# Key norms and gate sums moved from the chunks of a hybrid recurrent layer into its projection

## What is computed

```
x += 0.5 * post(SwiGLU_1(pre(x)))
h  = pre(x);  z = h @ w_in           # one combined projection
      gated DeltaNet (4 heads of 128), GLA (4 heads), Mamba-2 SSD (8 heads), merge gates
x += post(out(merge of the three branches by sigmoid gates of h))
x += 0.5 * post(SwiGLU_2(pre(x)))
```

```
def _l2norm(x):
    return x * rsqrt(sum(x*x, axis=-1) + 1e-6)
# DeltaNet, per chunk:  G = cumsum(g);  dec = exp(G_i - G_j)
#   A = strict(beta * (k k^T) * dec);  sol = (I + A)^-1 [beta v, beta e^G k]
#   u = sol_v - sol_k S;  o = (q e^G) S + ((q k^T) * dec) u
#   S = e^G_last S + (k e^(G_last - G))^T u
# Mamba-2 SSD: the same running sums, with dt * A as the gate
```

## Time and profile before

| | us |
|---|---|
| median of 3 runs (3424.24 to 3428.06) | 3427.71 |
| the profiled execution | 3428.86 |
| its span, first to last instruction | 3427.1 |
| PE busy | 3229.5 (94%) |
| DVE busy | 1315.3 (38%) |
| ACT busy | 778.4 (23%) |
| POOL busy | 1572.4 (46%) |
| mean granted clock of PE | 0.966 |
| projection of layer 0, its 40 windows and narrow stage | 480 to 711 |
| chunk stage of layer 0 | 711 to 1006 |
| chunk stage of layer 1, its chunks | 2410 to 2706 |

### The profile page before, as it was taken

How to read it: one execution, slowest core, us unless ns; L and a number is a source line. 1 busy time by engine, 2 the same in 40 slices (tenths; PEclk the granted TensorE clock), 3 DMA queues, 4 the chain that set the end, 5 groups by cost and what they waited for, 6 DMA issues and landing times. The chain is left out here.

```text
span 3427.1 us, 67666 instructions
## 1 busy us (share of the span) xinstructions
PE 3229.5 (94%) x26954; PEld 3108.2 (91%) x26954; DVE 1315.3 (38%) x2171; ACT 778.4 (23%) x1447; POOL 1572.4 (46%) x948
## 2 busy tenths in 40 slices
PE   7999989988889999999999999999888899899997
PEld 7999989977669998999999999899676799899997
DVE  3331065558752214331043310753676522233301
ACT  2111032234441112111021111332434311221100
POOL 4665546610016654655545654566000266545553
PEclk9999999998979999999999999999988899999999
DMA  3222222200042222222222222222001322212221
GB/s 124 88 86 85 69 77 86 92 1 1 29 145 87 87 88 68 86 86 85 76 78 88 90 80 69 82 87 73 1 2 70 118 87 90 89 62 86 89 82 65
DMA packets 77997, 259.88 MB, mean 76 GB/s; under 512 B 8576, under 2 KB 10624, under 8 KB 77056
## 3 DMA queue, kind: packets, MB, share of 16 engines
q1 hardware_dynamic: 77536, 256.90, 23.4%
q10 hardware_dynamic: 288, 0.49, 0.1%
HBM read 242.78 MB, written 14.58 MB: 75 GB/s over the span
## 5 line engine op out<-in xcount | busy, mean ns | idle before, releaser
L510 POOL TENSOR_SCALAR wh<-raw 128x1024 fp32r<-128x1024 f32 (+1 forms) x464 | 471.8, 1017 | 1757.3 <-PE ps L551 1161.6
L512 POOL TENSOR_TENSOR wl<-raw,wh 128x1024 fp32r<-128x1024 f32 (+1 forms) x464 | 1066.8, 2299 | 67.8 <-POOL wh L510 0.3
L547 PE MATMUL ps<-hh,wh 128*128 128x272 f32 x4768 | 999.4, 291 | 67.2 <-DVE hl L1767 44.5
L549 PE MATMUL ps<-hl,wh 128*128 128x272 f32 x4768 | 994.0, 289 | 0.0
L551 PE MATMUL ps<-hh,wl 128*128 128x272 f32 x4768 | 989.5, 289 | 0.0
L547 PEld LDWEIGHTS ps<-hh,wh 128*128 128x128 f32 x4768 | 755.9, 190 | 74.9 <-issue 59.3
L549 PEld LDWEIGHTS ps<-hl,wh 128*128 128x128 f32 x4768 | 753.3, 189 | 0.0
L551 PEld LDWEIGHTS ps<-hh,wl 128*128 128x128 f32 x4768 | 752.7, 189 | 0.0
L1776 DVE SCALAR_TENSOR_TENSOR f<-f,prm,rstd_post 128x544 f32<-128x544 f32 x48 | 43.7, 916 | 653.7 <-ACT rstd_post L1276 653.7
L547 PE MATMUL ps<-ah,wh 128*128 128x272 f32 x1408 | 294.5, 291 | 0.0
L549 PE MATMUL ps<-al,wh 128*128 128x272 f32 x1408 | 290.2, 287 | 0.0
(11 more groups left out here) (421 smaller groups left out, 3678.5 us busy)
## 6 DMA issues: line engine op xcount, KB each, us to landing
raw<-in_up SPq DMA_DIRECT2D x176, 512.0 KB, 3.5
raw<-in_win SPq DMA_DIRECT2D x80, 512.0 KB, 3.5
raw<-in_merge SPq DMA_DIRECT2D x96, 384.0 KB, 3.1
raw<-in_down SPq DMA_DIRECT2D x64, 512.0 KB, 3.5
raw<-in_down SPq DMA_DIRECT2D x32, 384.0 KB, 3.2
raw<-in_wout SPq DMA_DIRECT2D x16, 512.0 KB, 3.5
states<-in_in_gdn SPq DMA_DIRECT2D x2, 2048.0 KB, 8.1
proj<-in_in_ssd SPq DMA_DIRECT2D x2, 2048.0 KB, 12.4
```

The costliest lines, as they stand in the source:

```text
L510: pool.tensor_scalar(hi, src, 1.0, 1.0, MULT, MULT).then_inc(hi_done, 1)
L512: pool.tensor_tensor(lo, src, hi.bitcast(F32), SUB).then_inc(lo_done, 1)
L547: pe.matmul(out, high, mh_[:, c], start=a, stop=False)
L549: pe.matmul(out, high, ml_[:, c], start=False, stop=False)
```

## The change

1. `common` is gone from the chunks, with its instructions on PE, ACT and DVE.
2. **Keys and queries** are normalised in the projection, in place. Behind the conv tiles ACT loads its Ln/Exp table and squares the eight tiles (L1713) into rows of `proj` that are still unused; PE adds `key_sums(t)` (L1212) behind window 12 + t, in the PSUM slot that is free then; ACT takes Ln (L1721) and Exp (L1723); DVE multiplies the tiles in place.
3. **Gate sums** of all chunks are made near the projection's end: five transposes behind the first window of group 8 (`token_rows`), the running sums of 512 columns twice behind its third (`running_sums`), the sum rows behind the first of group 9 (`sum_rows`). ACT copies them out.
4. The chunks read `cm`, `tm_all`, `gc` and `rg` by chunk, and the keys and queries from `proj`. DeltaNet's spreads wait for the chunk before (`g_oc`, `g_s`). In the sample step `bx` is made first. The sample norm waits for two more things.
5. The projection's windows are written out from the fourth group on (28 of 40), and the three order strings are new.

The diff, cut to its core:

```diff
@@ PE, chunks
-            def common(step):
-                pe.wait_ge(both["cc"], value(pe, step.once + 1))
-                pe.transpose(ps[0:n, 2, 0:P], cc[:, 0:n], ident).then_inc(both["tmp"], 1)
...
-                for b in range(-(-w // 512)):
-                    c = min(512, w)
-                    last = pe.matmul(ps[:, b, 0:c], ones, sq8[:, b * 512:b * 512 + c], start=True, stop=True)
             def gdn(step):
-                pe.wait_ge(g_["brb"], value(pe, o + 1))
-                pe.wait_ge(both["rg"], further(pe, o + 1))
+                pe.wait_ge(g_["oc"], o + 1)
+                pe.wait_ge(g_["s"], o + 1)
...
@@ PE, projection
+            def key_sums(layer, t):
+                slot = (t + 2) % 4
+                pe.wait_ge(key_["sq"], layer * KEYS + t + 1)
+                pe.wait_ge(evict_done, layer * 40 + 12 + t + 3)
+                for h in range(2):
+                    last = pe.matmul(ps[:, 2 * slot + h, 0:HALF], ones, key_squares(t)[:, h * HALF:(h + 1) * HALF], start=True, stop=True)
+                last.then_inc(key_["ss"], 1)
+            def token_rows(layer):
...
+                for c in range(CHUNKS):
+                    pe.transpose(ps[:, 4, c * P:(c + 1) * P], cm[:, c * P:(c + 1) * P], ident)
+                pe.transpose(ps[0:SAMPLE, 5, 0:P], cm[:, SEQ:T], ident).then_inc(gate_["tr"], 1)
+            def running_sums(layer):
...
+                pe.matmul(ps[:, 0, :], tri, tm_all[:, :], start=True, stop=True)
+                pe.matmul(ps[:, 1, :], rev, tm_all[:, :], start=True, stop=True).then_inc(gate_["cum"], 1)
...
-                with pe.Fori(0, 10) as i:
+                with pe.Fori(0, 3) as i:
                     for j in range(4):
+                        window(i, j)
+                for t in range(KEYS + 2):
+                    if t >= 2:
+                        pe.wait_ge(key_["ln"], layer * KEYS + t - 1)
+                    window(3 + t // 4, t % 4)
+                    if t < KEYS:
+                        key_sums(layer, t)
...
+                window(8, 0)
+                token_rows(layer)
+                window(8, 1)
+                pe.wait_ge(gate_["tm"], layer + 1)
+                window(8, 2)
+                running_sums(layer)
+                window(8, 3)
+                pe.wait_ge(gate_["gc"], layer + 1)
+                window(9, 0)
+                sum_rows(layer)
+                window(9, 1)
+                pe.wait_ge(gate_["br"], layer + 1)
...
@@ ACT, projection
-                with act.Fori(0, 2) as i:
-                    direct_group(i, 3, LQ, ACT.Copy)
+                act.preload_act_table_set(LN_EXP)
+                act.wait_ge(csil_done, layer * CONV_TILES + KEYS + 2)
+                for t in range(2):
+                    square(t)
+                for t in range(KEYS):
+                    block_in(0, 3, t)
+                    act.activation(halves(proj[:, LQ + t, :]), pair(t % 4), ACT.Copy).then_inc(evict_done, 1)
+                    act.wait_ge(key_["ss"], layer * KEYS + t + 1)
+                    act.activation(halves(key_squares(t)), pair((t + 2) % 4), ACT.Ln, bias=epsc).then_inc(key_["ln"], 1)
+                    act.wait_ge(key_["ln"], layer * KEYS + t + 1)
+                    act.activation(key_squares(t), key_squares(t), ACT.Exp, scale=-0.5).then_inc(key_["rs"], 1)
+                    if t + 2 < KEYS:
+                        square(t + 2)
...
@@ DVE, projection
                     conv_group(i, 0, 0)
+                for t in range(KEYS):
+                    dve.wait_ge(key_["rs"], layer * KEYS + t + 1)
+                    dve.scalar_tensor_tensor(out=proj[:, GQ + t, :], in0=proj[:, GQ + t, :], scalar=GDN_SCALE if t < 4 else 1.0,
+                                             in1=key_squares(t), op0=MULT, op1=MULT).then_inc(key_["n"], 1)
                 narrow_columns(layer)
...
@@ DVE, chunks
-                dve.tensor_tensor(view(kn[:, 0:w], 4), proj[:, GK:GK + 4, step.cols], view(rs8[:, w:2 * w], 4), MULT)
-                dve.scalar_tensor_tensor(out=view(qn[:, 0:w], 4), in0=proj[:, GQ:GQ + 4, step.cols], scalar=GDN_SCALE,
-                                         in1=view(rs8[:, 0:w], 4), op0=MULT, op1=MULT).then_inc(g_["qk"], 1)
```

More of the change, by code:

```diff
@@ L679, in spread @@
-            def spread(bank, off, rowi, n):
-                return pe.matmul(ps[:, bank, off:off + n], cst[:, IDENT + rowi:IDENT + rowi + 1].to_broadcast([P, P]),
-                                 br[:, 0:n], start=True, stop=True)
+            def spread(bank, off, rowi, step):
+                return pe.matmul(ps[:, bank, off:off + step.n], cst[:, IDENT + rowi:IDENT + rowi + 1].to_broadcast([P, P]),
+                                 cm[:, step.cols], start=True, stop=True)
             def gdn(step):
@@ L1058, in ssd @@
                 for h in range(SSD_HEADS):
-                    last = spread(6 + h // 4, h % 4 * n, ROW_DT + h, n)
+                    last = spread(6 + h // 4, h % 4 * n, ROW_DT + h, step)
                 last.then_inc(s_["bc"], 1)
@@ L1681, in project @@
                     conv_group(i, 5, SX, 12)
-                for group, tile in ((7, GZ), (8, LG), (9, SZ)):
-                    direct_group(0, group, tile, ACT.Silu)
+                act.wait_ge(key_["n"], layer * KEYS + KEYS)
+                direct_group(0, 7, GZ, ACT.Silu)
+                for t in range(8):
+                    block_in(0, 8, t)
+                    act.activation(halves(proj[:, LG + t, :]), pair(t % 4), ACT.Silu).then_inc(evict_done, 1)
+                    if t == 0:
+                        act.wait_ge(gate_["tr"], layer + 1)
+                        act.activation(tm_all[:, :], ps[:, 4, :], ACT.Copy)
+                        act.activation(tms[0:SAMPLE, :], ps[0:SAMPLE, 5, 0:P], ACT.Copy).then_inc(gate_["tm"], 1)
+                    elif t == 2:
+                        act.wait_ge(gate_["cum"], layer + 1)
+                        for dst, bank in ((gc, 0), (rg, 1)):
+                            for at_, rows in gate_rows:
+                                m = rows.stop - rows.start
+                                last = act.activation(dst[:, 0:CHUNKS, at_:at_ + m],
+                                                      ps[:, bank, :].rearrange("p (c r) -> p c r", r=P)[:, :, rows], ACT.Copy)
+                        last.then_inc(gate_["gc"], 1)
+                    elif t == 4:
+                        act.wait_ge(gate_["row"], layer + 1)
+                        for r in (slice(0, 32), slice(64, P)):
+                            act.activation(cm[r, 0:SEQ], ps[r, 4, :], ACT.Copy)
+                            act.activation(cm[r, SEQ:T], ps[r, 5, P:P + SAMPLE], ACT.Copy)
+                        for at_, rows in gate_rows:
+                            m = rows.stop - rows.start
+                            last = act.activation(gc[0:SAMPLE, CHUNKS, at_:at_ + m], ps[0:SAMPLE, 5, rows], ACT.Copy)
+                        last.then_inc(gate_["br"], 1)
             def narrow_columns(layer):
@@ L1706, in _ @@
                 act.preload_act_table_set(LN_EXP)
+                act.wait_ge(gate_["gc"], layer + 1)
+                act.activation(rg[:, :, :], rg[:, :, :], ACT.Exp).then_inc(gate_["rg"], 1)
                 steps = steps_of(layer)
[L1708 removed]
+                together(SCALAR_ORDER, g=branch_of(gdn, gdn_sample, steps),
                          l=branch_of(gla, gla_sample, steps), s=branch_of(ssd, ssd_sample, steps),
@@ L2341, in sample_norm @@
                 dve.wait_ge(s_["yc"], step.once + 2)
+                dve.wait_ge(l_["vt"], step.once + 1)
+                dve.wait_ge(g_["s"], step.once + 1)
                 gated(step)
```

197 lines of the change are left out of this document (88 added, 109 removed).

## The result

| | before | changed |
|---|---|---|
| median of 20 runs, us | 3425.33 | 3434.11 |
| lowest and highest | 3419.21, 3429.53 | 3428.58, 3440.74 |
| the profiled execution | 3428.86 | 3434.35 |
| its span | 3427.1 | 3432.2 |
| PE busy | 3229.5 | 3217.7 |

The change makes the kernel **slower by 0.27%**: ratio 1.0027, 95% interval 1.0021 to 1.0033. Forecast was 0.3% faster. The two profiled executions differ by 5.1 us in span and the medians by 8.8 us: the profiled execution of the changed kernel took its median time, that of the kernel before 3.5 us more than its own.

The account below looks back on a forecast made before the run. PE was taken to bound the projection, and a chain passing between PE and DVE the chunks. Per layer +27.0 in the projection and -31.5 in the chunk stage gave -4.5, -9.0 in all: 3418.7 us, range 3399 to 3445.

Parts of the forecast that it names:

- The rival of PE's queue: Chunks: DVE's shorter chain finds PE occupied, so three chunks gain only 11.1 us; 3443.5 us in all, chance 0.20.
- The two marks: Where PE's queue decides: chunk gains under half of those forecast, and the sum changing sign at -16.5 for three chunks.
- my -21: Chunks 1 to 3: summed gain of 21.0 us a layer from the shorter DVE chain, bounds -11 and -24.
- The projection: Projection: 11.5 us of added PE work, 12.5 of waiting and 3 of half clock, +27.0 us a layer.
- The gap: Projection, before the first key sum: PE waits 12.5 us for ACT's square of tile 0, bounds 10.5 and 18.8.
- The rival stall of 18.8: Projection: if DVE's taps keep their earlier pace, the stall is 18.8 us, +6.3 a layer, 3431 us; chance 0.13.
- The heads of the chunks: Chunks 1 to 3, state update to xtb on DVE: 12.7, 10.6, 12.7 us in place of 17.9, 18.6, 21.7.
- One sign that I had named: Chunks: PE's wait for xtb, 24.3 us in eight chunks before, would be under 8 us in the run.
- What I leave off, 0.4 a chunk: Chunks 1 to 3: the only deduction for PE work standing behind the new xtb, 0.4 us a chunk.
- if those waits don't hold them: Chunks: GLA's start items, some 2.5 us of DVE, move ahead into waits; otherwise the chunk's end is late by as much.
- The sample step: Sample step: an earlier spread's difference and two norm operations leaving the way gain 8.5 us a layer, bounds -3 and -11.
- Chunk 0: First chunk: loses two norms of 512 columns, a copy and a wait for ACT, -2 us a layer.

Follow-up runs that it names:

- old_orders: The changed kernel with the three order strings of before, c taken out and one g added at the sample step; 3465.06 us, ratio 1.0103 to the kernel before.
- gla_back: late16 with GLA's start items of chunks 1 to 3 put back behind DeltaNet's state update on PE, ACT and DVE; 3439.56 us, ratio 1.0037 to before.
- late16: The changed kernel with two key sums behind each of windows 16 to 19, not one behind each of 12 to 19; 3408.77 us, ratio 0.9936 to before.
- sample_old: late16 with the order strings of before from the sample step's first letter of DeltaNet on; 3405.84 us, ratio 0.9942 to the kernel before.

## Why the prediction was wrong

The forecast was -4.5 us a layer; the trace has +2.1 and +3.1, the medians +4.4. Its sign was wrong. The range held the result, but none of the rivals gave it by its mechanism. The rival of PE's queue had the sign, 3443.5, but asked for chunks of 53 us and more with PE busy over 90%, and for 11.1 us of gain in three chunks: they take 51.2 to 52.1 us, PE was busy for 44.32 of 51.6, and they gained 17.7. (The two marks that I gave for it don't agree either: -16.5 is not half of my -21.)

*The projection*, +27.0, was right: 26.5 and 26.0. The gap was there, 13.9 for 12.5, with POOL silent in it; the clock cost 2.2 for 3; the work 10.4 for 11.5. That the sum came within 1 us is in part luck, since these misses cancel; counted from the first eviction it was 26.9 and 27.6, and 27.6 and 28.0 in the second execution. Window 12 had ended at 545.85, not at 547.1, and the first key sum began at 559.73 where I had 559.6. The rival stall of 18.8 fell with the row of the taps at 2.64. The Trainium skill's rule (GPSIMD Engine Reference, Specifications), that GpSimd contends with VectorE instructions with two SBUF inputs, agrees with these rows: the taps slow down beside POOL and speed up without it. The copy `cs_p` too took 0.16 without POOL and up to 2.37 beside it, though it has one input; the same section of the Trainium skill names a mode with two ports beside the two inputs, and whether the copy ran in it no row shows. The Trainium skill's rule of about 1.38 us more for each table switch (ScalarE: Activation LUTs, What ACT_TABLE_LOAD costs) does not show: the load began 0.02 us after the last SiLU, and the square 0.01 us after the load, at 559.02.

*The heads of the chunks*, 12.7, 10.6 and 12.7, were right: 12.2, 10.3, 12.2, a gain of 23.4 us in both layers. One sign that I had named failed all the same: PE's wait for `xtb` is 20.8 us in the run and not under 8. PE now stops for it 8.5 us after the update of chunk 0 (13.4 before) and waits 3.8 us (4.6 before): its own queue ahead of that wait got shorter with DVE's.

**The step that failed** is the one behind it: "What I leave off, 0.4 a chunk, is PE work that now stands behind the new xtb". It took the stretch from `xtb` to the next state update for unchanged. That stretch was 38.96, 38.41 and 37.08 us before and is 39.48, 41.75 and 39.03 now, **5.8 us** longer in both layers, for 1.2 allowed. It came with the new order and not with the removed instructions: in `old_orders`, which lacks the common stage but keeps the old strings, the three stretches are 114.2 in all, as before (114.5). Of it GLA's start items are 2.6 to 3.9: in `gla_back`, which has them behind the update, the stretches are 38.8, 38.6 and 39.1, 116.4 in all, against 119.0 in `late16` and 120.3 in its second execution. The rest, some 2, I can't put to one row; the new order has also moved norm operations. I had written that the items might make the end of the chunk late "if those waits don't hold them", and had given that no number. So the chunks gained 17.7 and not 21.0.

*The sample step* gained 5.4 and 2.2 us (3.7 and 3.3 in the other execution) for 8.5. Its head came as forecast: the difference L1972 starts 3.2 us after the update, 11.5 before. The gain was lost in the tail. Take the first `proj<-u_yo,ps` (L2329, L2277 before) as the border: DVE reached it at 973.4, 35.1 us after the update, before the change, and now at 969.9, 24.2 after, so 10.9 us of gain were there. Behind it the stretch was 32.6 us and is 38.1. Before, changed and `sample_old`, with the columns of the earlier trace rows:

```profile
973.40:1005.95 32.55, 21.19 (x182) 15.66 (x182) 29.93 (x55) 16.58 (x48) 5.24 (x4) 0.57 0.42 146
...
969.90:1008.05 38.15, 25.48 (x256) 19.33 (x255) 31.12 (x57) 20.96 (x60) 5.33 (x4) 0.55 0.29 105
...
967.36:999.39 32.03, 21.29 (x183) 15.66 (x183) 29.42 (x55) 16.61 (x48) 5.40 (x4) 0.56 0.40 148
```

PE has 4.3 us more work behind the border (256 instructions for 182), and DVE is idle for 7.0 us there instead of 2.6, in these waits of the changed kernel:

```profile
DVE proj L2343 <- PE ps L1158: 3.1, 2, 2.0
DVE hl L2424 <- ACT hh L1659: 2.2, 2, 2.0
DVE nt_s L2355 <- ACT nrs_s L1641: 1.5, 1, 1.5
```

The two halves of the step, us and PE's mean granted clock, layers 0 and 1:

| | update to border | clock | border to merge | clock |
|---|---|---|---|---|
| before | 35.1, 35.1 | 0.85, 0.85 | 32.6, 32.5 | 0.57, 0.57 |
| changed | 24.2, 27.3 | 1.00, 0.81 | 38.1, 38.1 | 0.55, 0.56 |
| changed, again | 25.8, 26.0 | 0.87, 0.87 | 38.2, 38.3 | 0.55, 0.55 |
| `late16` | 27.3, 27.3 | 0.81, 0.81 | 38.1, 38.3 | 0.57, 0.57 |
| `late16`, again | 24.2, 24.2 | 1.00, 1.00 | 38.1, 38.1 | 0.55, 0.55 |
| `sample_old` | 32.2, 29.6 | 0.84, 1.00 | 32.0, 32.1 | 0.56, 0.56 |
| `old_orders` | 36.4, 36.5 | 0.77, 0.77 | 31.9, 32.1 | 0.56, 0.56 |

In every profile, a stage with the new order of the sample step takes 38.1 to 38.3 us behind the border and a stage with the old one 31.9 to 32.6, at the same clock, so it is the order and not PE's low clock that made the tail longer. `sample_old` also shows what the order gave: at a clock of 1.00 the first half takes 29.6 with the old order and 24.2 with the new. It took some 5 us from one half and put 6 on the other. This is the second step that failed: I had the stretch behind the spread's difference only shorten, by the norm operations that leave it, and did not count the products that the new order moved there. Within one order what varies is the first half, and with it the clock: 24.2 us at 1.00, 25.8 and 26.0 at 0.87, 27.3 at 0.81. The 5.4 us gained in one layer and 2.2 in the other differ by just that. What makes the clock differ between executions stays open.

*Chunk 0* gained 1.4 and 3.0 for 2 (-0.2 and 2.9 in the other execution).

A layer's misses are thus 4.6 in the remainders, 3.1 to 6.3 in the sample step, and -0.5 to -1.0 in the projection; chunk 0 and the heads give a little back. They turned -4.5 into +2 to +3. Nor was the forecast far enough from zero to bear them: it was the difference of 27 and 31.5, each uncertain by more than it.

**A version that beats both** is `late16`: 0.6% faster than the kernel before in two sets of runs. Counted from the first eviction, its projection costs 11.8 to 12.0 us a layer more than before (two profiles) in place of 26.9 to 28.0, for the same stage.

## What to carry to other kernels

When work moves from a stage with slack into one where an engine is full, look first at who that engine will wait for there: three fifths of the price here, 16.1 of 26.5 us, were not the work but its position, and starting four windows later removed it. When a chain is shortened at its head, write down what was moved in front of it and price the whole period, from one update to the next, and not the head alone: both terms that failed here were stretches behind the head, taken as unchanged. Where an order is searched anew together with an edit, run the edit with the old order: here the order was worth more than the removed instructions.

## What the runs showed of the hardware

Stopping PE made DVE faster. PE's stop silenced POOL, and DVE's conv tile (pass, taps and copies) then took 3.4 us instead of 6.2, which shortened the wait that had caused it. The copy of 128x3 numbers took 2.35 us beside POOL and 0.16 without it. An fp32 product of 16 columns instead of 272 still took half as long: two pairs 0.96 us against 2.00, and the window around them grew by 0.89 against 1.76. And the stage of one program varied by up to 5.6 us between executions; in one stretch the time went with the granted clock, 24.2 us at 1.00 and 27.3 at 0.81.
